# First layer's output projection with its last two column quarters computed pair by pair, the fourth quarter's weights held beside the first two slots, and a new place for the turning of each pair

## Chip, cores and metric

One core of one Trainium2 chip runs the whole program. The metric is device time in microseconds. The kernel before has a median of 3025.3 us over three runs (3021.27 to 3028.36).

## The reference, cut to what matters

The program computes two transformer layers and then a second, different block; all data are float32. The change is between the two layers of the first block. For layer l, with rows h (16 meta rows and 1024 token rows, width 1024):

```
hn   = rmsnorm(h, norm_gain[l])            # x * rsqrt(mean(x*x) + 1e-6) * gain
proj = hn @ w_in[l]                        # q, k, v, gates, forget column
...                                        # attention, gives do, fo (512 wide each)
h    = h + concatenate([do, fo]) @ w_out[l]
```

What matters here is the last line for l = 0 and the first two for l = 1: output projection, residual add, row statistics, scaling, and the first products of the next layer.

## The kernel before, in words

Five engines run five instruction streams in order. Each wait is a semaphore that a helper `Count` names by a key. **TensorE** products are done three times (high by high, high by low, low by high parts of a float32 pair), by `mm3` at L597, recorded on L595; transposes are on L604.

**Weights.** The list `PLAN` gives the order in which 512 KB slices of weights are loaded. SyncE loads slice w into one of two float32 buffers (`W32`, slot w % 2) once slice w - 2 has been split (L2702 to L2705). ScalarE writes the rounded high part (`split_to`, L1203, recorded on L1214), VectorE the low part (L1778, on L1782), each into one of two slots of `WH`, `WL`. A slot is free when the products of the slice that had it are done (`W_OVER`). Slices in `ASIDE` go elsewhere: before the change only those of a later projection, "out2", through the table `PAIRED`.

**Output projection** (`tensor_out`, L830). There are nine row tiles: eight of 128 token rows and one of 16 meta rows; two tiles make a pair p = 0 to 3, and the meta rows are pair 4. The 1024 output columns are four quarters q of 256. Each quarter has two weight slices (kk = 0, 1), each of four 128-row chunks. One tile of one slice is 12 matmuls of 128x256, so a pair of a quarter is 48, and pair 4 is 24. Quarters 0 to 2 run all nine tiles for kk = 0, then all for kk = 1. Quarter 3 runs by pairs, in `PAIR_ORDER` = 4, 0, 1, 2, 3; behind the product of place i it turns (transposes) the normalised rows of the pair of place i - 2.

**PSUM banks.** `Banks.take` (L69) gives out, of the banks allowed, the one that was taken longest ago. Who takes a bank waits for the instruction that frees it. A pair's product holds one bank, until VectorE has added it to h (`add`, L2059, recorded on L2068, for the meta rows on L2072). Turning a pair takes eight banks, one for each 128 columns (`tensor_norm_fill`, L624); bank k is freed by the k-th VectorE instruction of `norm_fill` (L1819, recorded on L1825), which runs behind ScalarE's k-th (L1254, on L1259). In quarter 3 of the kernel before, turning may not use the banks that the remaining pairs hold. In the attention, products and small steps take banks 5, 6, 7 only; 0 to 4 belong to scores.

**Normalising a pair.** When all four quarters of a pair are added: ScalarE squares and sums its two tiles and takes the root (`norm_stats`, L1247, recorded on L1226 and L1228), VectorE takes the reciprocal and scales both tiles (`norm_scale`, L1809, on L1788 and L1817), TensorE turns them, ScalarE and VectorE write the high and low parts to `AH`, `AL`. Written order: ScalarE, for each place i of `PAIR_ORDER`: statistics of place i, then the fill of place i - 1 (for i = 1 to 3). VectorE: the add of quarter 3 one place ahead, scale of place i, fill of place i - 1. The statistics are ready only one place later than the add, and the turning one more.

**Into layer 1.** `first_projections` (L376) writes the order by hand: chunk 0 of q (352 columns, needs pairs 4, 0 and 1), the fill of pair 2, chunk 0 of k, the fill of pair 3, chunks 1 and 2 of q, and so on. Position coding of a q or k chunk (`rope`) runs one matmul, one VectorE, one GpSimd and further steps beside the next products. GpSimd also stores the finished rows of h tile by tile (L2605), once quarter 3 of a pair is added.

Of the kernel before, what the change touches and what calls it, by code (L numbers as in the profile page):

```python
# [92 lines left out]
def build(nc, A, S, O):  # L93

    ctx = ExitStack()
    with ctx:
# [27 lines left out]
        with ExitStack() as first_block:  # L124
# [3 lines left out]
            QH, QL, KH, KL = (own(n, [128, 2, L], F32R) for n in ("QH", "QL", "KH", "KL"))  # L128
# [36 lines left out]
        with ExitStack() as folded_rows:  # L165
# [7 lines left out]
            EXH = spot("EXH", 22304 - 20256, [128, 2, 1024])[:, :, :]  # L173
# [73 lines left out]


        PLAN, WI = [], {}
        PAIRED = {"out2": [(EXH[:, k, :], EXL[:, k, :]) for k in range(2)], }  # L250

        def weight(key, src, split=True):
            WI[key] = len(PLAN)
# [116 lines left out]
        def chunk(g, kind, ci):  # L370
            steps = [("unit", g, kind, ci, k) for k in range(KT)]
            if kind in "qk" and g < 4:
                steps += [("late", n, (what, g, kind, ci)) for n, what in ((2, "rope"), (4, "rope_add"), (7 if g == 0 else 9, "rope_end"))]
            return steps

        def first_projections(l):  # L376

            if l == 0:
                return (chunk(0, "q", 0) + [("fill", 2), ("stats", 3)] + chunk(0, "k", 0) + chunk(0, "q", 1) + [("fill", 3)] + chunk(0, "k", 1)
                        + [("set_up",)] + chunk(0, "q", 2) + [("split", NEXT[WI[l, 0, "k"]])] + chunk(0, "k", 2) + projections(l, 0, "f") + projections(l, 0, "v"))  # L380
            return (chunk(0, "q", 0) + [("fill", 2)] + chunk(0, "k", 0) + [("fill", 3)] + chunk(0, "q", 1) + chunk(0, "q", 2)
                    + [("split", NEXT[WI[l, 0, "k"]])] + chunk(0, "k", 1) + chunk(0, "k", 2) + projections(l, 0, "f") + projections(l, 0, "v"))

        def attention_steps(l):
# [795 lines left out]
        def tensor(e):  # L1180
            banks.__init__()
            e.wait_ge(*const_in[0].at("all"))
            for p in PAIR_ORDER[:3]:
                tensor_norm_fill(e, 0, p)
            tensor_attention(e, 0)
            tensor_out(e, ("out", 0), OUT_COLS[0], lambda kt: [(o_lo, (0, kt))], lambda q, p: (out_added, (("out", 0), q, p)),
                       PAIR_ORDER, lambda i, among: tensor_norm_fill(e, 1, PAIR_ORDER[i - 2], among) if i >= 2 else None)
            tensor_attention(e, 1)
            between = {0: lambda: tensor_mod(e), 1: lambda: tensor_fill(e, "ctxrows", XC, fill_tb)}
            tensor_out(e, ("out", 1), OUT_COLS[1], lambda kt: [(o_lo, (1, kt))], lambda q, p: (out_added, (("out", 1), q, p)),  # L1190
                       after=lambda i, among: tensor_norm_fill(e, "lat", 0, among) if i == 2 else None,
                       between=lambda q: between[q]() if q in between else None)
            tensor_ctx(e)
            tensor_mixer(e)
            tensor_fourier(e)
            tensor_ffn(e)
# [3 lines left out]
        def scalar(e):  # L1200
# [46 lines left out]
            def norm_stats(l, p):  # L1247
                def ready(i):
                    t = PAIRS[p][i]
                    return [(x_in[p], PAIRS[p][-1])] if l == 0 else [(out_added, (("out", 0), 3, t // 2))]  # L1250
                t0, n = PAIRS[p][0], len(PAIRS[p])
                statistics((l, p), [N_TILES[t] for t in PAIRS[p]], ready, RSTD[:, t0:t0 + n], FIN[:, 0:1024] if (l, p) == (0, 3) else JK)
# [8 lines left out]
            def norm(l):  # L1261
                if l == 0:
                    norm_stats(0, 4)
                    norm_stats(0, 0)
                    norm_fill(0, 4)
                    norm_stats(0, 1)
                    norm_fill(0, 0)
                    split_to(WI[0, 0, "q"])
                    norm_fill(0, 1)
                    norm_stats(0, 2)  # L1270
                    split_to(WI[0, 0, "k"])
                    return
                for i, p in enumerate(PAIR_ORDER):
                    norm_stats(l, p)
                    if i == 3:
                        split_to(WI[l, 0, "k"])
                    if 1 <= i < 4:
                        norm_fill(l, PAIR_ORDER[i - 1])

            def attention(l):  # L1280
# [128 lines left out]
                        do[st[0]](*st[1:])  # L1409

            def out_splits(name):
                for q in range(4):
                    for kk in range(2):
                        split_to(WI[name, q, kk] + ((q, kk) < (3, 1)))

            def sum_h(q, p):

# [357 lines left out]
        def vector(e):  # L1775
# [52 lines left out]
            def norm(l, add=None):  # L1828

                if l == 0:  # L1830
                    norm_scale(0, 4)
                    norm_scale(0, 0)
                    norm_fill(0, 4)
                    norm_scale(0, 1)
                    norm_fill(0, 0)
                    split_to(WI[0, 0, "q"])
                    norm_fill(0, 1)
                    norm_scale(0, 2)
                    split_to(WI[0, 0, "k"])
                    return  # L1840
                add(0)
                for i, p in enumerate(PAIR_ORDER):
                    if i < 4:
                        add(i + 1)
                    norm_scale(l, p)
                    if i == 3:
                        split_to(WI[l, 0, "k"])
                    if 1 <= i < 4:
                        norm_fill(l, PAIR_ORDER[i - 1])

            def attention(l):
# [204 lines left out]
            def out(l):  # L2056
                name = ("out", l)

                def add(q, p):  # L2059
                    c = slice(256 * q, 256 * q + 256)  # L2060
                    b = banks.place.get((name, q, p), 0)
                    e.wait_ge(*out_mm.at((name, q, p)))
                    if p < 4:
                        if q == 0:
                            for t in (2 * p, 2 * p + 1):
                                e.wait_ge(*tile_in[t].at(1 + l))
                        o = HT[:, 2 * p:2 * p + 2, c]
                        e.tensor_tensor(o, o, bank(b).rearrange("p (a b) -> p a b", a=2), ALU.add).then_inc(*out_added.mark((name, q, p)))  # L2068
                    else:
                        if q == 0:  # L2070
                            e.wait_ge(*tile_in[8].at(1))
                        e.tensor_tensor(HM[0:NM, c], HM[0:NM, c], bank(b)[0:NM, 0:256], ALU.add).then_inc(*out_added.mark((name, q, p)))  # L2072

                if l == 0:
                    for q in range(4):
                        for kk in range(2):
                            split_to(WI[name, q, kk] + ((q, kk) < (3, 1)))
                        if q < 3:
                            for p in range(5):
                                add(q, p)  # L2080
                    norm(1, lambda i: add(3, PAIR_ORDER[i]))
                    return

                def gain(q, p):

                    c = slice(256 * q, 256 * q + 256)
                    o = HT[:, 2 * p:2 * p + 2, c]
                    e.wait_ge(*squared.at(("h", q, 2 * p + 1)))
                    if q == 0 and p == 0:
                        e.wait_ge(*fg_in.at(0))  # L2090
                    e.tensor_tensor(o, o, FG[:, c].unsqueeze(1).broadcast_to([128, 2, 256]), ALU.mult).then_inc(*fg_mul.mark((q, p)))

                for q in range(4):
                    if q == 1:
                        inverse("ctx", RSTD[:, 16:18])
                        e.wait_ge(*rstd.at("ctx"))
                        for t in range(2):
                            e.tensor_scalar(XC[t], XC[t], RSTD[:, 16 + t:17 + t], None, ALU.mult).then_inc(*scaled.mark(("ctxrows", t)))
                        modulation()
                    if q == 2:  # L2100
                        fill("ctxrows", [(128, 0), (128, 128)], None, TBc, CAH, CAL)
                    split_to(WI[name, q, 1])
                    if q:
                        gain(q - 1, 2)
                        gain(q - 1, 3)
                    if q < 3:
                        split_to(WI[name, q + 1, 0])
                        add(q, 0)
                        add(q, 1)
                        gain(q, 0)  # L2110
                        add(q, 2)
                        gain(q, 1)
                        add(q, 3)
                between_blocks(lambda p: add(3, p), lambda p: gain(3, p))
# [742 lines left out]
```

## Time and profile before

| what | value |
|---|---|
| median of three runs | 3025.3 us |
| the profiled execution, its own time | 3023.28 us |
| its span (first to last instruction) | 3021.5 us |
| TensorE matmul busy | 2834.5 us, 94% |
| VectorE busy | 1545.5 us, 51% |
| ScalarE busy | 1021.3 us, 34% |
| mean granted TensorE clock | 0.977 |

The time beside the span, 1.8 us, is launch and end. Times in the rows below are from the span's start. The output projection of layer 0 begins at about 807 us and layer 1's first product at 931.67 us. A timeline row gives the start, the length, engine, line and operation; in brackets stand the idle time before it and what ended that. The length of a matmul contains its pipeline, so the pace is read from start to start.

### The profile page before, as it was taken

Reading aid. Unit: us, or ns where it says so; the run is one execution under the profiler, and the core shown is the slowest. Engines: PE = TensorE matmul, PEld = TensorE weight load, DVE = VectorE, ACT = ScalarE, POOL = GpSimd, SP = SyncE. Lnnn points to the kernel's source line nnn. Section 1 sums busy time; section 2 is a strip of 40 time slices with the busy share of each in tenths; the row PEclk is TensorE's granted clock in tenths of the full one; section 3 lists DMA queues with packets and bytes.
Section 4 is the critical chain, followed back from the end, with each engine's and each line's share of the span. In section 5 each row is a group of like instructions: output and inputs, shape, how many; then the busy total and the mean of one; then the engine's idle time right before and its main releaser. Section 6 shows DMA issues by size and latency. Waiting matters only on the chain.

```text
span 3021.5 us, 43091 instructions
## 1 busy us (share of the span) xinstructions
PE 2834.5 (94%) x17460; PEld 2423.9 (80%) x17460; DVE 1545.5 (51%) x2800; ACT 1021.3 (34%) x1960; POOL 209.5 (7%) x295
## 2 busy tenths in 40 slices
PE   6899989999898889999999898999999999999999
PEld 6777777888798777877887797888898888888887
DVE  5655555545524655654455447555436444445335
ACT  5333333323214333333233355222334222223233
POOL 1000000000101100000000106000012000000000
PEclk9999999999899999999999899999999999999999
DMA  4112221120322212222221314111332111111113
GB/s 130 39 55 60 59 55 55 55 62 29 116 61 71 54 39 63 55 59 63 73 52 43 118 55 133 49 43 46 127 100 71 49 49 49 42 49 49 49 63 133
DMA packets 205397, 198.10 MB, mean 66 GB/s; under 512 B 7286, under 2 KB 181686, under 8 KB 205198
## 3 DMA queue, kind: packets, MB, share of 16 engines
q1 hardware_dynamic: 187344, 134.27, 16.8%
q0 software_dynamic: 17856, 61.07, 5.5%
q8 instruction: 141, 2.31, 0.3%
q14 instruction: 56, 0.46, 0.0%
HBM read 162.73 MB, written 32.58 MB: 65 GB/s over the span
## 4 chain that ended last, share of the span: by engine, by line
PE 79%; DVE 10%; ACT 5%; issue 4%; DMA 2%; POOL 1%; SPq 0%; ACTq 0%; DVEq 0%; POOLq 0%
PE PS L595 75%; PE PS L604 4%; DVE WL L1782 1%; DVE ST L1969 1%; DMA W<-in_w_in 1%; ACT top L1362 1%; ACT WH L1214 1%; DVE AL L1825 1%; DVE AL L2152 0%; DMA R<-in_k_fg 0%; DMA TMP<-s_os 0%; DVE V L1957 0%; DVE AL L2044 0%; DVE top L1985 0%; DVE top L1982 0%
## 5 line engine op out<-in xcount | busy, mean ns | idle before, releaser
L595 PE MATMUL PS<-AH,WH 128*128 128x512 f32 (+3 forms) x2624 | 993.7, 379 | 20.5 <-DVE AL L1825 13.8
L595 PE MATMUL PS<-AL,WH 128*128 128x512 f32 (+3 forms) x2624 | 923.6, 352 | 0.0
L595 PE MATMUL PS<-AH,WL 128*128 128x512 f32 (+3 forms) x2624 | 920.9, 351 | 0.0
L595 PEld LDWEIGHTS PS<-AH,WH 128*128 128x128 f32 x2624 | 500.5, 191 | 103.2 <-issue 21.9
L595 PEld LDWEIGHTS PS<-AL,WH 128*128 128x128 f32 x2624 | 501.4, 191 | 49.7 <-issue 1.7
L595 PEld LDWEIGHTS PS<-AH,WL 128*128 128x128 f32 x2624 | 499.9, 191 | 43.0
L1782 DVE TENSOR_TENSOR WL<-W,WH 128x1024 fp32r<-128x1024 f32 x186 | 228.5, 1230 | 325.4 <-ACT WH L1214 325.2
L595 PE MATMUL PS<-WH,AH 128*128 128x256 f32 (+1 forms) x1088 | 350.7, 322 | 11.4 <-DVE WL L1782 5.3
L595 PE MATMUL PS<-WH,AL 128*128 128x256 f32 (+1 forms) x1088 | 348.7, 320 | 0.0
L595 PE MATMUL PS<-WL,AH 128*128 128x256 f32 (+1 forms) x1088 | 348.6, 320 | 0.0
L1214 ACT ACTIVATE WH<-W 128x1024 fp32r<-128x1024 f32 x186 | 195.5, 1052 | 280.4 <-PE PS L595 256.4
L1969 DVE TENSOR_REDUCE ST<-PS 128x1 f32<-128x784 f32 (+8 forms) x272 | 187.9, 732 | 152.3 <-PE PS L595 151.8
L604 PE MATMUL PS<-ident,top 128*128 128x128 f32 (+2 forms) x1132 | 189.8, 284 | 59.1 <-issue 21.3
L595 PEld LDWEIGHTS PS<-WH,AH 128*128 128x128 f32 x1088 | 208.4, 192 | 31.2 <-DVE R L2206 5.1
L1362 ACT ACTIVATE top<-PS,ST 128x784 f32<-128x784 f32 (+8 forms) x272 | 194.2, 721 | 91.8 <-DVE ST L1969 60.2
L595 PEld LDWEIGHTS PS<-WH,AL 128*128 128x128 f32 x1088 | 208.8, 192 | 15.2
L595 PEld LDWEIGHTS PS<-WL,AH 128*128 128x128 f32 x1088 | 208.6, 192 | 15.0
L604 PEld LDWEIGHTS PS<-ident,top 128*128 128x128 f32 (+2 forms) x1132 | 133.5, 136 | 94.2 <-issue 36.9
L595 PE MATMUL PS<-top,V 128*64 128x256 f32 (+6 forms) x1176 | 187.4, 381 | 7.0 <-DVE top L2006 4.2
L595 PEld LDWEIGHTS PS<-top,V 128*64 128x64 f32 (+3 forms) x1176 | 121.3, 157 | 76.0 <-issue 44.9
L1701 ACT ACTIVATE R<-PS,R 128x512 f32<-128x512 f32 x88 | 68.5, 779 | 299.5 <-PE PS L595 299.5
L2489 DVE SCALAR_TENSOR_TENSOR R<-PS,R 128x504 f32<-128x504 f32 x88 | 65.4, 743 | 191.9 <-ACT R L1701 191.9
(326 smaller groups left out, 3243.8 us busy)
## 6 DMA issues: line engine op xcount, KB each, us to landing
W<-in_w_in SPq DMA_DIRECT2D x94, 512.0 KB, 7.7
W<-in_w_ada SPq DMA_DIRECT2D x48, 512.0 KB, 3.6
W<-in_w_up SPq DMA_DIRECT2D x44, 512.0 KB, 3.7
W<-in_w_out SPq DMA_DIRECT2D x24, 512.0 KB, 3.4
W<-in_w_down SPq DMA_DIRECT2D x22, 512.0 KB, 3.6
R<-s_xs POOLq DMA_DIRECT2D x16, 512.0 KB, 6.7
s_adap<-AST POOLq DMA_DIRECT2D x48, 128.0 KB, 7.9
top<-in_x SPq DMA_DIRECT2D x8, 512.0 KB, 9.3
```

The lines of the kernel that those rows point to most:

```text
L595: return e.matmul(out, lhsT, rhs, start=start, stop=stop, skip_group_check=True)
L604: return e.transpose(out, in_, ident[0:k, 0:k])
L1214: e.activation(high(v), W32[:, s, :], ACT.Copy).then_inc(*w_hi.mark(v))
L1362: e.activation(P[0:rows, P_SLOT[u], 0:W], PSf[0:rows, o:o + W], ACT.Exp, bias=st[:, 0:1], accum_out=st[:, 1:2]).then_inc(*exped.mark(u))
L1701: e.activation(dst[:, c:c + n], bank(b), ACT.Identity, scale=CW[:, 1, jj:jj + 1], bias=CW[:, 3, jj:jj + 1]).then_inc(*conv_a.mark((j, ab, ...
L1782: e.tensor_tensor(low(v), W32[:, slot32(v), :], f(high(v)), ALU.subtract).then_inc(*w_lo.mark(v))
L1825: e.scalar_tensor_tensor(lo, bank(b)[:, 0:n], COLS[:, 8 * l + k:8 * l + k + 1], f(hi), ALU.mult, ALU.subtract).then_inc(*fill_lo.mark((l, ...
L1969: e.tensor_reduce(ST[0:rows, ST_SLOT[u], 0:1], PSf[0:rows, o:o + W], AX.X, ALU.max, negate=True).then_inc(*row_max.mark(u))
L2489: e.scalar_tensor_tensor(d3[:, :, 1:64], o3[:, :, 0:63], CW[:, 0, jj:jj + 1], d3[:, :, 1:64], ALU.mult, ALU.add).then_inc(*conv_v.mark((j, ...
```

## The change

- `PAIRED` now also holds the projection of layer 0, with the q buffers of the attention (`QH`, `QL`, idle at that time) as the place of the two slices of quarter 3. So the order of `PLAN` for this projection becomes (0,0), (0,1), (1,0), (3,0), (1,1), (3,1), (2,0), (2,1).
- `tensor_out`, which already has the paired form, now runs quarters 2 and 3 as: pair p of quarter 2, pair p of quarter 3, then `after`. Each takes its bank just ahead of its product, out of all eight, and `after` may use all eight.
- Turning is at place i - 1 in place of i - 2, for i = 1 to 4. Pair 2 is thus turned in the projection, and its fill leaves layer 1's list.
- ScalarE and VectorE follow: VectorE adds both quarters of place i, scales it, and then fills place i - 1. The splits of layer 1's first two slices stand at place 4 between the adds of quarters 2 and 3 (ScalarE: before the statistics of place 4).

```
-        PAIRED = {"out2": [(EXH[:, k, :], EXL[:, k, :]) for k in range(2)], }
+        QHf, QLf = (x[:, :, :].rearrange("p a b -> p (a b)") for x in (QH, QL))
+        SIDES = [(QHf[:, 1024 * k:1024 * k + 1024], QLf[:, 1024 * k:1024 * k + 1024]) for k in range(2)]
+        PAIRED = {("out", 0): SIDES, "out2": [(EXH[:, k, :], EXL[:, k, :]) for k in range(2)], }
...
-            return (chunk(0, "q", 0) + [("fill", 2)] + chunk(0, "k", 0) + [("fill", 3)] + chunk(0, "q", 1) + chunk(0, "q", 2)
+            return (chunk(0, "q", 0) + chunk(0, "k", 0) + [("fill", 3)] + chunk(0, "q", 1) + chunk(0, "q", 2)
...
-                       PAIR_ORDER, lambda i, among: tensor_norm_fill(e, 1, PAIR_ORDER[i - 2], among) if i >= 2 else None)
+                       PAIR_ORDER, lambda i, among: tensor_norm_fill(e, 1, PAIR_ORDER[i - 1], among) if i else None)
...
                 for i, p in enumerate(PAIR_ORDER):
+                    if i == 4:
+                        split_to(WI[l, 0, "k"])
                     norm_stats(l, p)
-                    if i == 3:
-                        split_to(WI[l, 0, "k"])
-                    if 1 <= i < 4:
+                    if i:
                         norm_fill(l, PAIR_ORDER[i - 1])
...
             def out_splits(name):
-                for q in range(4):
-                    for kk in range(2):
-                        split_to(WI[name, q, kk] + ((q, kk) < (3, 1)))
+                split_to(WI[name, 2, 1])
...
-                add(0)
                 for i, p in enumerate(PAIR_ORDER):
-                    if i < 4:
-                        add(i + 1)
+                    add(2, p)
+                    if i == 4:
+                        split_to(WI[l, 0, "k"])
+                    add(3, p)
                     norm_scale(l, p)
-                    if i == 3:
-                        split_to(WI[l, 0, "k"])
-                    if 1 <= i < 4:
+                    if i:
                         norm_fill(l, PAIR_ORDER[i - 1])
...
                 if l == 0:
-                    for q in range(4):
-                        for kk in range(2):
-                            split_to(WI[name, q, kk] + ((q, kk) < (3, 1)))
-                        if q < 3:
-                            for p in range(5):
-                                add(q, p)
-                    norm(1, lambda i: add(3, PAIR_ORDER[i]))
+                    split_to(WI[name, 3, 0])
+                    for p in range(5):
+                        add(0, p)
+                    split_to(WI[name, 2, 0])
+                    for p in range(5):
+                        add(1, p)
+                    split_to(WI[name, 2, 1])
+                    norm(1, add)
                     return
```

## Rows read from the trace of the kernel before

**Rows 1.** The page: span, TensorE's share, the chain that ended last.

```profile
span 3021.5 us, 43091 instructions
PE 2834.5 (94%) x17460; PEld 2423.9 (80%) x17460; DVE 1545.5 (51%) x2800; ACT 1021.3 (34%) x1960; POOL 209.5 (7%) x295
...
PE 79%; DVE 10%; ACT 5%; issue 4%; DMA 2%; POOL 1%; SPq 0%; ACTq 0%; DVEq 0%; POOLq 0%
```

**Rows 2.** Stretches: busy PE, PEld, DVE, ACT, POOL, granted clock, DMA share, GB/s.

```profile
825.00:889.00 64.00, 63.69 (x538) 63.69 (x539) 15.45 (x20) 5.24 (x5) 0.00 (x0) 1.00 0.26 85
...
905.00:925.00 20.00, 16.34 (x122) 15.51 (x122) 9.57 (x27) 10.63 (x28) 2.72 (x5) 0.91 0.27 106
925.00:940.00 15.00, 10.02 (x61) 9.52 (x61) 9.92 (x20) 9.04 (x23) 1.34 (x2) 0.89 0.55 141
...
950.00:970.00 20.00, 20.00 (x122) 19.19 (x121) 9.33 (x16) 5.85 (x11) 6.38 (x5) 1.00 0.16 33
970.00:990.00 20.00, 20.00 (x131) 19.79 (x131) 9.71 (x11) 7.75 (x10) 0.00 (x0) 1.00 0.23 41
```

**Rows 3.** Timeline of TensorE around the five turnings and into layer 1.

```profile
907.35 0.37 PE L604 MATMUL PS<-ident,OTt 16*128 16x16 f32 x2 [1.38 <-DVE AL L1825]
907.65 0.51 PE L595 MATMUL PS<-WH,AH 128*128 128x256 f32 x1
...
918.02 0.36 PE L595 MATMUL PS<-WH,AH 128*128 128x256 f32 x1
...
931.67 0.66 PE L595 MATMUL PS<-AH,WH 128*128 128x352 f32 x1 [4.90 <-DVE AL L1825]
...
937.16 1.91 PE L604 MATMUL PS<-ident,V 128*128 128x128 f32 x16
939.15 0.43 PE L595 MATMUL PS<-AH,WH 128*128 128x352 f32 x1
...
940.72 0.86 PE L595 MATMUL PS<-TMP,rotm 128*128 128x352 f32 x2 [0.33 <-DVE AL L1825]
...
944.34 0.27 PE L604 MATMUL PS<-ident,GT 128*128 128x128 f32 x1
...
947.99 0.40 PE L595 MATMUL PS<-AH,WH 128*128 128x344 f32 x1 [1.74 <-DVE AL L1825]
...
1023.18 0.38 PE L604 MATMUL PS<-ident,top 128*16 128x128 f32 x2 [4.48 <-issue]
```

**Rows 4.** Timeline of VectorE: the adds of quarter 3, scalings and fills.

```profile
899.25 0.69 DVE L2068 TENSOR_TENSOR top<-top,PS 128x512 f32<-128x512 f32 x1 [5.27 <-PE PS L595]
...
904.94 0.69 DVE L2068 TENSOR_TENSOR top<-top,PS 128x512 f32<-128x512 f32 x1 [4.16 <-PE PS L595]
...
905.74 1.42 DVE L1817 TENSOR_SCALAR V<-top,SM 128x1024 f32<-128x1024 f32 x2
907.07 1.25 DVE L1825 SCALAR_TENSOR_TENSOR AL<-PS,COLS,AH 128x16 fp32r<-128x16 f32 x8
915.16 0.69 DVE L2068 TENSOR_TENSOR top<-top,PS 128x512 f32<-128x512 f32 x1 [6.84 <-PE PS L595]
...
917.30 3.22 DVE L1825 SCALAR_TENSOR_TENSOR AL<-PS,COLS,AH 128x256 fp32r<-128x256 f32 x8
924.00 0.69 DVE L2068 TENSOR_TENSOR top<-top,PS 128x512 f32<-128x512 f32 x1 [3.48 <-PE PS L595]
```

**Rows 5.** Timeline of ScalarE: statistics of pair 0 (the first and the root).

```profile
899.98 1.06 ACT L1226 ACTIVATE TMP<-top 128x1024 f32<-128x1024 f32 x1 [3.20 <-DVE top L2068]
...
902.40 0.30 ACT L1228 ACTIVATE SM<-SM 128x2 f32<-128x2 f32 x1
```

**Rows 6.** Stretches for TensorE alone: busy, granted clock, DMA share, GB/s.

```profile
907.00:908.00 1.00, 0.65 (x4) 0.88 0.85 348
...
911.00:912.00 1.00, 1.00 (x9) 0.92 0.06 20
...
1028.00:1030.00 2.00, 2.00 (x6) 0.50 0.00 0
```

## The prediction, made before the change was run

> **What bounds the kernel now.** I read the page first: TensorE is busy 94% of the span and has 79% of the chain that ended last [rows 1]. Then the stretches of this stage: inside the quarters TensorE is full (63.69 of 64 us), but around the turnings it is busy 16.34 of 20 and 10.02 of 15 us, with the granted clock at 0.91 and 0.89; from 950 us on it is full again for 40 us [rows 2]. So what this stage is worth is read from TensorE's own gaps and clock, and what TensorE loses by 948 us reaches the end, as nothing behind it has slack to take it up before 990 us. The timeline of TensorE shows the gaps, those of VectorE and ScalarE what they wait for [rows 3 to 5].
>
> **How a turning costs time before.** A turning wants eight banks and there are eight. I measure from the start of the add that follows a pair's last product to TensorE's next product. Pair 4 is turned from 904.94: the seventh turn must take again a bank that the same turning filled, and waits 1.38 us for the first fill of VectorE, which stands behind the scaling of the next pair (905.74, 1.42 us); next product 907.65, so 2.71 us [rows 3, 4]. Pair 0: 915.16 to 918.02, 2.86 us. Pair 1: 924.00 to 931.67, 7.67 us; layer 1's first chunk needs all eight fills, and two splits stand ahead of them. Pair 2, in layer 1: 937.16 to 939.15 and then 0.33 of wait, 2.3 us. Pair 3: 944.34 to 947.99, 3.65 us, 1.74 of it a wait for the fill that frees a bank. Sum **19.2 us**. The clock fell to half (1.2 of 2.4 GHz) after the turning of pair 4 and came back in 911 to 912; the 48 matmuls there took 7.51 us (907.65 to 915.16) where a pair takes 5.69 (899.25 to 904.94): about 1.65 us lost [rows 3, 4, 6]. After the gap of 4.90 us the same: the mean clock of 0.89 over 15 us is 1.65 us of work lost [rows 2]. In both together **3.3 us**.
>
> **Part 1: the order of products and weights.** The number of products is the same: two quarters, 4.5 pairs each at 5.69 us, 51.2 us. The extra waits for weights on each tile are on semaphores long passed; I take 0.2 us in all. The two slices of quarter 3 are split during quarter 1 and the loads shift by one place. VectorE's adds of quarter 0 wait behind the split of (3,0), some microseconds; TensorE asks for a bank of quarter 0 only at the fourth pair of quarter 1, three pairs of 12 matmuls a tile after its start (8.5 us), so I cost that at nothing; a load later than that would be waited for (rival d). The short wait for the second slice ahead of the first by-pairs quarter (pair 4 gives only 12 matmuls of cover for one split of ScalarE and one of VectorE) moves from quarter 3 to quarter 2 and keeps its price. The slices of layer 1 come earlier. GpSimd's stores of h keep their place behind each pair. Nothing gained, nothing lost: **+0.2 us**.
>
> **Part 2: turning one place sooner.** This is where the change decides. Behind the products of place i TensorE turns place i - 1 into all eight banks, and the next product takes the bank taken longest ago: the first of that turning. It is freed by VectorE's first fill. That fill stands on VectorE behind the adds and the scaling of place i, and this scaling needs ScalarE's statistics of place i, which can begin only when TensorE has just ended place i. Before, the statistics of a place ran beside the next place's products; now they are in front of it. The chain from the add's start a, from rows of pair 0: ScalarE starts at a + 0.73 (899.98 - 899.25), root at a + 3.15 (902.40) [rows 4, 5]; the reciprocal 0.3 later and the scaling 0.2 behind that, as between 904.94 + 0.69 and 905.74 nothing else is slow; scaling to the first fill takes 1.33 (905.74 to 907.07) [rows 4]. So the first fill starts at a + 5.0. A small fill is 0.16, a large one 0.40 (3.22 / 8), and TensorE follows 0.04 later. Products resume at **a + 5.25** behind the turning of pair 4, and at **a + 5.46** behind those of pairs 0 and 1. Sixteen turns are 1.9 us [rows 3], so the idle time is 3.6 us, and 4.4 behind pair 4.
>
> **Part 3: into layer 1.** Pair 2 is turned at place 4, again into eight banks. Chunk 0 of q may use 5, 6, 7 only. I followed the order in which banks are taken from the end of the attention (2, 1, 4, 0, 3, then the three others): the turning of pair 2 begins with bank 3, and its second bank is the first of the three. So chunk 0 waits for the second fill: a + 5.0 + 0.81 + 0.04 = **a + 5.87**, in place of 7.67 before. Its weights are split beside pair 3 of quarter 3 and are early. Then chunk 0 of k follows at once, and pair 3 is turned: 3.65 us as before, plus up to 0.6, since ScalarE's end of the position coding of q now falls on the end of chunk k, without the turning of pair 2 between them: 4.25.
>
> **The sum.** After: 5.25 + 5.46 + 5.46 + 5.87 + 4.25 = 26.3 us; before 19.2; **+7.1 us**. The clock: four gaps of 3.6 to 4.4 us with TensorE idle where before it fell twice. The gap of 4.90 was followed by half clock, that of 1.74 was not (the stretch at 950 us is at 1.00) [rows 2, 3]; mine are nearer the first. Two more falls at 1.65: **+3.3 us**. With part 1, +10.6; I take **+10**, as the 0.6 at pair 3 may not come. The profiled execution took 3023.3 us, so 3033; it stood 2 us under the median of 3025.3, and the median should go to about **3035**.
>
> The Trainium skill, "TensorE: Matmul & The Clock Gate", section "HAM oscillation — how this bites in real kernels", says that a gap repeated in every step is paid again in every step, since the array restarts at half clock each time. By it all four gaps would bring a fall, the 3.3 us above; the two gaps at 907 and 931 us agree, that each of the new ones does so no row can show yet.
>
> **Rivals.** (a) *Turning is hidden, faster.* Banks rotate, and the fills of a turning run beside the next products. Then only the turns themselves stay: 0.9 + 1.9 + 1.9 + 1.9 + 4.25 = 10.9 us in place of 19.2, and no clock falls: -8.3 - 3.3 = -11.6, so 3013.7. (0.9 for the small turning: its last bank waits for the add, 0.69 us [rows 4].) It decides if the first fill can start within the 1.9 us of the turns, or break-even if it starts about 2.5 us sooner than a + 5.0. Against it: ScalarE's two squares alone last from a + 0.73 to a + 3.15, and the wait of 1.38 us at 907.35 shows that a bank not yet filled from does stop TensorE. Chance 0.06. The Trainium skill's "Perfetto Trace Analysis", section "Optimizing Tensor Performance", says that product groups should rotate through different banks so that emptying one overlaps the next; by it the change would go this way. The same page, "Identifying Performance Opportunities", reads the same gap repeating on the bounding engine as too little PSUM for the next tile; that speaks against the change, and the wait at 907.35 agrees.
>
> (b) *The clock falls no more often than before, or layer 1 takes some up.* +3 to +6.6: 3028 to 3032. For it: a fall needs not follow each gap. The chunks to 990 us leave no slack [rows 2], later stalls might. Chance 0.17.
>
> (c) *Half clock lasts twice as long.* After the 4.48 us gap at 1023.18 the clock was still 0.50 in 1028 to 1030 [rows 3, 6]. If that happens in each of four gaps, +6.6 more: about 3042. Chance 0.12.
>
> (d) *The new order of weights starves quarter 1.* A late (3,0) delays VectorE's adds; it must be over 8 us late. +2 us or more; chance 0.03.
>
> (My forecast: the remaining 0.62.) What a measurement of this kernel can tell from no change is 0.2%, 6 us. Slower than that: the forecast, (c), (d), and a small part of (b): 0.77. Within it: most of (b): 0.15. Faster: (a) and a little for what I don't see: 0.08. Range: the low end takes in (b) nearly whole, 3027; the high end (c), 3043. Left out are (a) and the ends.
>
> **What would show it.** Right: TensorE idle 3.5 to 4.5 us three times between its pairs, each ended by VectorE's L1825, with half clock after each; ScalarE's squares of a pair at the same time as TensorE's turns of the pair before; layer 1's chunk 0 of q starting 5.9 us behind the last add; the stretch from the end of quarter 1 to chunk 1 of q about 10 us longer than before. Wrong: gaps under 2 us there (then rival a), or the stage longer by 10 us and the whole not (then something later had slack).

## The result, and the profile after

The changed kernel is **slower by 0.39%**: the ratio to the kernel before is 1.0039, 95% interval 1.0028 to 1.0049; medians of seven runs each are 3034.9 and 3023.1 us. The profiled execution took 3035.3 us against 3023.3, 12.0 us more. The page of the kernel after shows the same work in a longer span, with TensorE's busy time almost as before (2835.9 against 2834.5 us); helpers moved by two lines (products are now recorded on L597, turning on L606).

```profile
span 3033.5 us, 43095 instructions
PE 2835.9 (93%) x17460; PEld 2428.1 (80%) x17460; DVE 1545.2 (51%) x2800; ACT 1021.3 (34%) x1960; POOL 209.0 (7%) x295
```

The page can't say where 12 us went. The stretches can. These are the kernel after, cut at the ends of its pairs (busy time of PE, PEld, DVE, ACT, POOL, then granted clock, DMA share, GB/s):

```profile
882.00:902.00 20.00, 15.44 (x113) 15.16 (x112) 4.64 (x14) 3.91 (x13) 1.09 (x2) 0.83 0.13 53
902.00:922.00 20.00, 16.17 (x115) 15.94 (x114) 6.13 (x14) 5.50 (x13) 1.05 (x2) 0.83 0.13 53
922.00:941.00 19.00, 15.17 (x118) 14.93 (x117) 8.56 (x16) 7.71 (x16) 1.05 (x2) 0.91 0.22 68
941.00:960.00 19.00, 13.22 (x74) 12.54 (x72) 8.66 (x21) 9.49 (x24) 1.99 (x3) 0.82 0.33 98
960.00:990.00 30.00, 29.77 (x180) 28.79 (x181) 10.91 (x20) 7.32 (x15) 6.53 (x5) 1.00 0.15 36
```

Four stretches of 19 to 20 us in a row, each with 3.8 to 5.8 us in which TensorE does nothing, and each with a mean clock of 0.82 to 0.91. Before, two stretches looked so [rows 2]. TensorE's timeline names what ended each gap:

```profile
887.48 0.58 PE L597 MATMUL PS<-WH,AH 128*128 128x256 f32 x1 [4.31 <-DVE AL L1825]
901.26 1.91 PE L606 MATMUL PS<-ident,V 128*128 128x128 f32 x16
906.99 0.58 PE L597 MATMUL PS<-WH,AH 128*128 128x256 f32 x1 [3.83 <-DVE AL L1825]
...
926.96 0.58 PE L597 MATMUL PS<-WH,AH 128*128 128x256 f32 x1 [3.83 <-DVE AL L1825]
...
946.06 0.63 PE L597 MATMUL PS<-AH,WH 128*128 128x352 f32 x1 [4.26 <-DVE AL L1825]
...
953.07 0.75 PE L597 MATMUL PS<-TMP,rotm 128*128 128x352 f32 x2
...
956.58 0.27 PE L606 MATMUL PS<-ident,GT 128*128 128x128 f32 x1
...
960.23 0.40 PE L597 MATMUL PS<-AH,WH 128*128 128x344 f32 x1 [1.74 <-DVE AL L1825]
```

Each gap is ended by L1825, VectorE's fill, the instruction that gives a bank of the turning back. VectorE's own timeline shows why it comes so late, and ScalarE's shows what it waits for in turn:

```profile
863.90 0.41 DVE L2071 TENSOR_TENSOR OTt<-OTt,PS 16x256 f32<-16x256 f32 x1 [0.73 <-PE PS L597]
...
882.19 0.69 DVE L2067 TENSOR_TENSOR top<-top,PS 128x512 f32<-128x512 f32 x1 [4.98 <-PE PS L597]
885.66 0.17 DVE L1788 RECIPROCAL SM<-SM 128x2 f32<-128x2 f32 x1 [2.78 <-ACT SM L1230]
885.86 1.42 DVE L1817 TENSOR_SCALAR V<-top,SM 128x1024 f32<-128x1024 f32 x2
887.20 1.22 DVE L1825 SCALAR_TENSOR_TENSOR AL<-PS,COLS,AH 128x16 fp32r<-128x16 f32 x8
...
901.46 0.69 DVE L2067 TENSOR_TENSOR top<-top,PS 128x512 f32<-128x512 f32 x1 [4.98 <-PE PS L597]
...
906.46 3.22 DVE L1825 SCALAR_TENSOR_TENSOR AL<-PS,COLS,AH 128x256 fp32r<-128x256 f32 x8
...
921.42 0.69 DVE L2067 TENSOR_TENSOR top<-top,PS 128x512 f32<-128x512 f32 x1 [4.98 <-PE PS L597]
...
940.08 0.69 DVE L2067 TENSOR_TENSOR top<-top,PS 128x512 f32<-128x512 f32 x1 [2.21 <-PE PS L597]
```

```profile
882.91 1.06 ACT L1228 ACTIVATE TMP<-top 128x1024 f32<-128x1024 f32 x1 [8.88 <-DVE top L2067]
...
885.34 0.29 ACT L1230 ACTIVATE SM<-SM 128x2 f32<-128x2 f32 x1
885.54 1.41 ACT L1261 ACTIVATE AH<-PS,COLS 128x16 fp32r<-128x16 f32 x8
```

Read them together. Pair 0's last product ends at 882.19, the add starts; ScalarE had been idle for 8.88 us and begins the squares only at 882.91; VectorE waits 2.78 us for the root, scales for 1.4 us, and only then (887.20) fills the pair turned before. TensorE resumes at 887.48. From each add to the next product: 5.29, 5.53 (901.46 to 906.99), 5.54 and 5.98 us (940.08 to 946.06). Behind the turning of pair 3 it is 3.65 us, as before.

I call **stage** the stretch from the last add of quarter 1 to the first product of chunk 1 of q. After, it is 960.23 - 863.90 = 96.33 us. Before, that add starts at 863.94 and the chunk at 947.99 [rows 3], 84.05 us. The stage is longer by 12.3 us, the execution by 12.0: within that difference of 0.3 us, the loss is all here.

### The profile page after: what moved, and what is told of

It reads as the page before. It is cut to its first block, busy times and chain, and to the rows that moved or that the text cites. A ratio compares the mean times of both kernels' runs of the same rounds, so it can differ in the third digit from the quotient of the medians.

```text
span 3033.5 us, 43095 instructions
## 1 busy us (share of the span) xinstructions
PE 2835.9 (93%) x17460; PEld 2428.1 (80%) x17460; DVE 1545.2 (51%) x2800; ACT 1021.3 (34%) x1960; POOL 209.0 (7%) x295
## 4 chain that ended last, share of the span: by engine, by line
PE 79%; DVE 9%; ACT 5%; issue 4%; DMA 2%; POOL 1%; SPq 0%; ACTq 0%; DVEq 0%; POOLq 0%
PE PS L597 75%; PE PS L606 4%; DMA W<-in_w_in 2%; DVE ST L1968 1%; DVE WL L1782 1%; ACT top L1364 1%; ACT WH L1216 1%; DVE AL L2152 0%; ACT TMP L1228 0%; DVE AL L1825 0%; DMA R<-in_k_fg 0%; DMA TMP<-s_os 0%; DVE V L1956 0%; DVE top L1984 0%; DVE AL L2043 0%
## 5 line engine op out<-in xcount | busy, mean ns | idle before, releaser
L597 PE MATMUL PS<-AH,WH 128*128 128x512 f32 (+3 forms) x2624 | 992.9, 378 | 19.8 <-DVE AL L1825 13.1
L597 PE MATMUL PS<-AL,WH 128*128 128x512 f32 (+3 forms) x2624 | 923.6, 352 | 0.0
L597 PE MATMUL PS<-AH,WL 128*128 128x512 f32 (+3 forms) x2624 | 921.8, 351 | 0.0
L597 PEld LDWEIGHTS PS<-AH,WH 128*128 128x128 f32 x2624 | 500.6, 191 | 101.4 <-issue 21.0
L597 PEld LDWEIGHTS PS<-AL,WH 128*128 128x128 f32 x2624 | 501.5, 191 | 49.5 <-issue 1.2
L597 PEld LDWEIGHTS PS<-AH,WL 128*128 128x128 f32 x2624 | 499.9, 191 | 43.0
L597 PE MATMUL PS<-WH,AH 128*128 128x256 f32 (+1 forms) x1016 | 333.0, 328 | 24.0 <-DVE AL L1825 12.0
L597 PE MATMUL PS<-WH,AL 128*128 128x256 f32 (+1 forms) x1016 | 330.5, 325 | 0.0
L597 PE MATMUL PS<-WL,AH 128*128 128x256 f32 (+1 forms) x1016 | 330.5, 325 | 0.0
L606 PE MATMUL PS<-ident,top 128*128 128x128 f32 (+2 forms) x1132 | 190.0, 284 | 61.0 <-issue 23.6
L597 PEld LDWEIGHTS PS<-WH,AH 128*128 128x128 f32 x1016 | 197.4, 194 | 44.3 <-DVE AL L1825 12.5
L606 PEld LDWEIGHTS PS<-ident,top 128*128 128x128 f32 (+2 forms) x1132 | 134.4, 137 | 95.2 <-issue 39.0
L597 PEld LDWEIGHTS PS<-WH,AL 128*128 128x128 f32 x1016 | 197.4, 194 | 15.2
L597 PEld LDWEIGHTS PS<-WL,AH 128*128 128x128 f32 x1016 | 197.4, 194 | 15.0
L597 PE MATMUL PS<-top,V 128*64 128x256 f32 (+6 forms) x1176 | 187.5, 381 | 7.0 <-DVE top L2005 4.2
L597 PEld LDWEIGHTS PS<-top,V 128*64 128x64 f32 (+3 forms) x1176 | 121.4, 158 | 76.1 <-issue 45.1
```

Source lines behind the costliest of these rows:

```text
L597: return e.matmul(out, lhsT, rhs, start=start, stop=stop, skip_group_check=True)
L606: return e.transpose(out, in_, ident[0:k, 0:k])
```

## The experiments

All are compared with the kernel before by the ratio of their times, and by their stage, read as above from one profiled execution each. The edits are shown against the changed kernel, cut ("...") and with some lines told in a comment.

| kernel | ratio, 95% interval | stage, us |
|---|---|---|
| before | 1 | 84.05 |
| changed | 1.0039 (1.0028 to 1.0049) | 96.33 |
| e1, by pairs, turned two places behind | 1.0003 (0.9995 to 1.0012) | 84.13 |
| e2, fill first | 0.9961 (0.9950 to 0.9973) | 70.74 |
| e3, two blocks to a bank | 0.9956 (0.9944 to 0.9968) | 68.69 |
| e4, turned again | 1.0024 (1.0015 to 1.0033) | 91.04 |
| e5, fill first on VectorE only | 1.0020 (1.0010 to 1.0031) | 90.05 |
| e6, banks reserved | 1.0040 (1.0026 to 1.0053) | 97.05 |
| e7, turned between | 0.9955 (0.9942 to 0.9967) | 70.62 |
| e8, between, two to a bank | 0.9952 (0.9940 to 0.9965) | 68.23 |

The stage's difference and the whole's agree within about 2 us in each: what is lost or won here reaches the end.

**e1: is it the order of products and weights, or the turning?** TensorE turns place i - 2 again, and the order on ScalarE and VectorE and the place of layer 1's splits follow the kernel before:

```
-  ... chunk(0, "q", 0) + chunk(0, "k", 0) + [("fill", 3)] ...
+  ... chunk(0, "q", 0) + [("fill", 2)] + chunk(0, "k", 0) + [("fill", 3)] ...
-  tensor_norm_fill(e, 1, PAIR_ORDER[i - 1], among) if i else None
+  tensor_norm_fill(e, 1, PAIR_ORDER[i - 2], among) if i >= 2 else None
   # VectorE: adds of both quarters one place ahead; splits at place 3 behind scale and statistics
```

> Part 1 of the change alone: quarters 2 and 3 by pairs and the weights in q's place, but turning stays two places behind, the fill of pair 2 stays in layer 1 and VectorE adds one place ahead, as before the change. If the loss is all in turning one place sooner, this takes as long as the kernel before, within 2 us (resumes at about 2.4 and 2.7 us behind the add, 7.7 into layer 1). If the new order of products and weights costs something itself, it is slower than before by more than 3 us.

Ratio 1.0003. TensorE's waits in e1 (engine and line, who was waited for: us in total, times, longest):

```profile
PE PS L597 <- DVE AL L1825: 10.1, 4, 6.0
PE PS L597 <- DVE WL L1782: 1.0, 1, 1.0
```

In the changed kernel the first of these rows has 18.0 us in five waits:

```profile
PE PS L597 <- DVE AL L1825: 18.0, 5, 4.3
```

So q's place for the weights, the new order of loads and the pairs of two quarters together cost nothing that can be measured. All the loss is in turning one place sooner, with the order on ScalarE and VectorE that goes with it. The equality is one of sums. In e1 products resume 2.41 and 2.66 us behind the turnings of pairs 4 and 0, a little sooner than before (2.71 and 2.86), 7.67 into layer 1 as before, and the half clock behind that last gap lasts longer (mean clock 0.85 in 922 to 932 and 0.80 in 932 to 942, against 0.98 and 0.85). So e1 bounds the cost of the new order of products and weights to about 1 us, an estimate from these differences, and not to 0.1.

**e2: the order on ScalarE and VectorE.**

```
   # in both engines, at each place i
-  norm_stats(l, p)            # VectorE: norm_scale(l, p)
   if i:
       norm_fill(l, PAIR_ORDER[i - 1])
+  norm_stats(l, p)            # VectorE: norm_scale(l, p)
```

> The changed kernel with one edit: at each place ScalarE and VectorE do the fill of the pair before ahead of the statistics and the scaling of the new pair. Theory (the gap is statistics and scaling standing in front of the fill that frees a bank): products resume 2.0 us behind the add in place of 5.3 to 5.5, layer 1's chunk 0 at 2.0 in place of 6.0, no half clock in the stage; 15 us less idle and some 9 us less at half clock, so about 24 us under the changed kernel and 12 under the one before, 3011. Rival (the fills themselves, 3.0 us on ScalarE and 3.2 on VectorE, are too slow for eight banks): products resume at 4 us or later, and at most 6 us are won.

The stage is 25.6 us shorter than the changed kernel's, ratio 0.9961 to the kernel before. TensorE, ScalarE and VectorE at the second turning:

```profile
892.89 1.91 PE L606 MATMUL PS<-ident,V 128*128 128x128 f32 x16
894.55 0.37 PE L597 MATMUL PS<-WH,AH 128*128 128x256 f32 x1
```

```profile
893.30 3.03 ACT L1261 ACTIVATE AH<-PS,COLS 128x256 fp32r<-128x256 f32 x8 [8.56 <-PE PS L606]
896.18 1.11 ACT L1228 ACTIVATE TMP<-top 128x1024 f32<-128x1024 f32 x1
```

```profile
893.09 0.69 DVE L2067 TENSOR_TENSOR top<-top,PS 128x512 f32<-128x512 f32 x1 [4.98 <-PE PS L597]
893.81 3.23 DVE L1825 SCALAR_TENSOR_TENSOR AL<-PS,COLS,AH 128x256 fp32r<-128x256 f32 x8
```

The fill starts 0.7 us behind the add in place of 5.0, and products resume at 1.46 us in place of 5.53, without a wait. That is even less than the 2.0 expected: the turning itself begins before the add. Into layer 1 it is 1.71 us (919.27 to 920.98). The granted clock is 1.00 in every stretch from 864 to 972, so the half clock is gone with the gaps. ScalarE's squares now follow the fill, beside the next products, where they hold up nobody. The rival (fills too slow for eight banks) falls: they take 3.0 and 3.2 us but the first of them frees its bank before TensorE asks for it.

**e3: are all eight banks part of it?** A turning puts blocks k and k + 1 into one bank, ScalarE and VectorE read them there; statistics and scaling still come first.

```
-  each = 1 if l in (0, 1) else 2
+  each = 1 if l == 0 else 2
   # the fills: bank of the even block, columns from 256 * (k % 2),
   # VectorE waits for ScalarE's part of both blocks
```

> The changed kernel with its order of work, but a turning puts two blocks of 128 columns into one bank, so it takes four banks in place of eight; ScalarE and VectorE still do statistics and scaling first. Theory (TensorE stops only because all eight banks are taken): products resume 2 us behind the add though the fills still start at 5 us, and some 20 to 24 us are won against the changed kernel. Rival (the order on ScalarE and VectorE alone sets the gap, whatever the banks): products still resume at about 5.5 us and nothing is won.

```profile
892.91 1.91 PE L606 MATMUL PS<-ident,V 128*128 128x128 f32 x16
894.57 0.37 PE L597 MATMUL PS<-WH,AH 128*128 128x256 f32 x1
```

```profile
893.11 0.69 DVE L2069 TENSOR_TENSOR top<-top,PS 128x512 f32<-128x512 f32 x1 [4.98 <-PE PS L597]
...
898.11 2.05 DVE L1827 SCALAR_TENSOR_TENSOR AL<-PS,COLS,AH 128x256 fp32r<-128x256 f32 x5
```

VectorE's fill still starts 5.0 us behind the add (898.11), yet TensorE goes on at 1.46 us, sooner than the 2 expected. Ratio 0.9956; the stage is 27.6 us shorter than the changed kernel's, more than the 20 to 24 expected, and 1.7 us of that is the wait behind the turning of pair 3 in layer 1, which is gone too. So the gap needs both: a late fill, and a turning that holds every bank. Taking away either one takes away the gap.

**e4: the clock.** Work is added to fill the gap: the transposes of pairs 0, 1, 2 are done twice, those of pair 4 six times, into the same place.

```
+  for again in range(1 if l != 1 or p == 3 else 6 if p == 4 else 2):
       for i, x in enumerate(tiles):
```

> The changed kernel with work added in the gap: in the projection each transpose of pairs 0, 1 and 2 is done twice, those of pair 4 six times, into the same place. The products still resume at 5.3 to 5.5 us behind the add, but TensorE idles 1.9 us in place of 3.8. If the idle time brings the half clock, the pairs behind the gaps run at their 11.4 us again in place of 13.1 to 14.4, and the whole is 7 to 9 us faster than the changed kernel, though it does more. If the half clock has another cause, or costs nothing in the end, the time is that of the changed kernel or up to 6 us more.

```profile
881.89 3.32 PE L606 MATMUL PS<-ident,OTt 16*128 16x16 f32 x48
...
906.36 0.38 PE L597 MATMUL PS<-WH,AH 128*128 128x256 f32 x1 [2.08 <-DVE AL L1826]
...
923.55 0.38 PE L597 MATMUL PS<-WH,AH 128*128 128x256 f32 x1 [2.08 <-DVE AL L1826]
...
941.19 0.40 PE L597 MATMUL PS<-AH,WH 128*128 128x352 f32 x1 [2.52 <-DVE AL L1826]
```

```profile
884.00:886.00 2.00, 1.20 (x17) 0.67 0.91 367
886.00:888.00 2.00, 0.72 (x3) 0.50 0.39 158
...
906.00:908.00 2.00, 1.64 (x13) 1.00 0.03 8
...
944.00:946.00 2.00, 2.00 (x9) 0.50 0.04 16
```

The columns of the second fence are TensorE's busy time, granted clock, DMA share and GB/s. With 2.08 us of gap in place of 3.83, the clock stayed at 1.00 (2.4 GHz) behind the turnings of pairs 0 and 1, and the 96 products there took 11.65 and 11.66 us (906.36 to the add at 918.01, 923.55 to 935.21) in place of 14.43 and 13.12. It still fell to 0.50 (1.2 GHz) around the turning of pair 4 and within layer 1's first chunk, behind a gap of 2.52 us. The fall at pair 4 does not follow the gap there (885.2 to 887.28, 2.08 us): the mean of 0.67 over 884 to 886 puts it at about 884.7, while the 48 small transposes (881.89 to 885.21) still ran. The kernel does more and is faster than the changed one: 5.3 us in the stage, 4.5 us by the ratios, whose intervals touch, so the stage is the firmer number. That is under the 7 to 9 us expected, because two of the four falls stayed: 13.54 us for the place behind pair 4 (887.28 to the add at 900.82) is still 1.9 over 11.65.

**e5: how the 5 us are made up.** Only VectorE's order is that of e2; ScalarE keeps statistics first.

> The changed kernel with half of e2: only VectorE does its fill ahead of the scaling; ScalarE keeps its statistics in front of its own fill. By the chain (statistics end at 3.4 us behind the add, then ScalarE's first fill, then VectorE's) products resume at 3.9 us behind large turnings and 3.7 behind the small one, in place of 5.5 and 5.3: 6.5 us less idle over four gaps, and one or two half clocks fewer, so 7 to 11 us under the changed kernel, near the one before. If ScalarE's part alone set the gap (the scaling was hidden), nothing is won; if VectorE's alone, as much as in e2.

```profile
885.40 0.39 PE L597 MATMUL PS<-WH,AH 128*128 128x256 f32 x1 [2.95 <-DVE AL L1825]
...
902.97 0.38 PE L597 MATMUL PS<-WH,AH 128*128 128x256 f32 x1 [2.67 <-DVE AL L1825]
```

The adds start at 881.48 and 898.59, so products resume at 3.92 and 4.38 us; I had said 3.7 and 3.9. The chain that I wrote down had ScalarE's first fill and then VectorE's behind statistics that end at 3.4 us, but 3.9 has room for only one of the two. Of the 5.53 us behind a large turning, VectorE's scaling in front was 1.15, ScalarE's statistics in front 2.9 (4.38 to e2's 1.46), and 1.46 is the turning and its start. The ratio, 1.0020, is 5.7 us under the changed kernel, less than the 7 to 11 expected. Products resumed 4.9 us sooner in sum, not 6.5, and the two gaps of 2.67 us, like those of 2.95 and 3.11, were still followed by half clock.

**e6: is it the choice of banks?** The banks of the next pair's two products are taken ahead of the turning, which then has six.

```
+  if name == ("out", 0) and i < 4:
+      hold(2, order[i + 1])
+      hold(3, order[i + 1])
-  after(i, ALL)
+  after(i, [b for b in ALL if b not in the two just held])
```

> The changed kernel with the banks of the next pair's two products taken ahead of the turning, which then has six, as the kernel before had in its last quarter. If stopping TensorE is a matter of which instruction takes the last bank, this helps: products resume at 2 us. If it is that the first fill starts only at 5.0 us, whoever needs a bank waits for it: now the seventh turn, and products resume at 5.8 us or so, 0 to 2 us slower than the changed kernel.

```profile
885.40 0.42 PE L606 MATMUL PS<-ident,OTt 16*128 16x16 f32 x2 [4.32 <-DVE AL L1830]
904.24 1.11 PE L606 MATMUL PS<-ident,V 128*128 128x128 f32 x4 [4.27 <-DVE AL L1830]
```

Now the transposes wait (L606), for the same instruction and no shorter than the products did (4.32 and 4.27 us against 4.31 and 3.83). Products resume 5.64 and 6.31 us behind the add, where 5.8 was expected; the ratio is 1.0040 and the stage 0.7 us longer than the changed kernel's. It is the late fill that counts, not who takes the last bank. This is the wait of 1.38 us at 907.35 in the kernel before [rows 3], grown by the statistics.

**e7 and e8: a version that beats both.** Fill first, and a pair is turned between the next pair's two quarters (`middle`), where its scaling is just done; e8 adds two blocks to a bank.

```
-  PAIR_ORDER, lambda i, among: tensor_norm_fill(...) if i else None)
+  PAIR_ORDER, middle=lambda i: tensor_norm_fill(e, 1, PAIR_ORDER[i - 1]) if i else None)
   # VectorE: add(2, p), fill of place i - 1, [splits], add(3, p), norm_scale(l, p)
```

> A version meant to be faster: fill first as in e2, and each pair is turned between the next pair's quarter 2 and quarter 3, 5.7 us behind its own last product, when its scaling (5.0 us) is just done. No turning is left behind the last product, so layer 1's chunk 0 starts at once. Four turnings still cost TensorE 0.5 to 1.9 us each. Expected: e2's time or 0 to 3 us less, 3007 to 3010; if the scaling comes too late, a wait of under 1 us at each turning.

> e7 with e3's two blocks to a bank. Banks are then short nowhere: the wait of 1.7 us for a bank behind the turning of pair 3 in layer 1 goes too. Expected 1 to 2 us under e7, about 14 us under the kernel before. If banks were not what was waited for there, the time of e7.

```profile
888.65 1.91 PE L606 MATMUL PS<-ident,V 128*128 128x128 f32 x16
...
934.27 0.40 PE L597 MATMUL PS<-AH,WH 128*128 128x344 f32 x1 [1.74 <-DVE AL L1825]
```

The place is right by a hair: in e7 the scaling of pair 0 starts at 886.84 and lasts 1.42 us, and its turning starts at 888.65 without a wait. Ratios 0.9955 and 0.9952. The stage is 0.12 us shorter than that of e2 (70.62), so the place wins nothing over e2; e8's two blocks to a bank win 2.4 us in the stage, among them the 1.74 us wait that the row above still shows. e2, e3, e7 and e8 can't be told apart by their ratios, whose intervals overlap; all four beat both kernels. e2 and e3 are the smallest steps from the changed kernel: e2 moves one line on each of two engines, e3 keeps the order and packs the banks.

## Why the prediction was right, point by point

- **Part 1 at +0.2 us.** e1 shows it: 84.13 us of stage against 84.05. The late split of (3,0) that rival (d) feared held up nothing; TensorE's one wait for weights in the stage is 0.99 us, as before, one quarter sooner.
- **Part 2, the chain behind the add.** Said: fill from a + 5.0, products at a + 5.25 and 5.46. Measured: the fill at 5.01 and 5.00, products at 5.29, 5.53, 5.54. e2 and e5 show the two parts of the chain, e3 the banks' part. The rows of the kernel before held all of it, because the same instructions ran there in another order.
- **Part 3, layer 1.** Said a + 5.87, measured 5.98, so the bank found by following the order of taking was right. Behind pair 3 I had 4.25, "up to 0.6" more than before; it was 3.65. The end of q's position coding did not get in the way.
- **The turnings together.** Said 26.3 against 19.2, +7.1. Measured 5.29 + 5.53 + 5.54 + 5.98 + 3.65 = 26.0, +6.8.
- **The clock, mis-sized.** This is the term of the sum that was off by most. Said two more falls at 1.65 us, +3.3. There were two more, but they cost more each. A full-clock place takes 11.66 us (e4); the three places behind gaps took 13.98, 14.43 and 13.12, so 2.3, 2.8 and 1.5 us lost. Chunk 0 of q (24 products, 0.161 us each at full clock, 4.0 with the start) took 6.0 (946.06 to the rope matmul at 953.07, less six products of k in front of it), 2.0 lost. Sum 8.6 us. Before, on the same measure, 1.5 at 907.65 to 915.16 and 1.5 in chunk 0: 3.0. The term is +5.6 and not +3.3. With 6.8 it makes 12.4, where the stage measured 12.3.
- **Why it was mis-sized.** I had priced a fall by its shortest examples. Reckoned from the means of stretches of 1 and 2 us, the half clock lasted about 3.4 us in both falls before (some 907.8 to 911.1 and 931.6 to 935.0), and in the changed kernel about 6.8 us in three and 3.4 in one. So what rival (c) assumed, twice as long, came true in three of four, but its +6.6 us did not: up to 2 us of each half-clock stretch lay over idle time, where it costs nothing, and a product at half clock starts every 0.213 us in place of 0.119 and not at twice the time. Of its 6.6 us, 2.0 came (8.6 against the forecast's 6.6). The second 1.65 us was read from a mean clock over a stretch with idle time in it; it fitted because that fall began only with the products.
- **The total.** Said +10, from a sum of +10.6; measured +12.0. The turnings were 0.3 us too high and the clock 2.3 too low, and part 1 cost nothing that can be measured. The larger term was right, and that kept the total near.
- **Rival (a)** needed the first fill within the 1.9 us of the turns. It starts at 5.0. But its price was nearly right for a kernel in which the turning is hidden: e2 is 0.39% under the kernel before, 11.8 us, and e3 0.44%, 13.3 us, where the rival said 11.6. The closeness is in part luck, as it priced the turning of pair 3 at 4.25 us, and e2 has 3.65 there.
- **Rival (b)** falls: all four gaps had a fall in them or right behind them, and nothing later took the loss up. The changed kernel's 12.3 us in the stage is 12.0 at the end.

The Trainium skill's "TensorE: Matmul & The Clock Gate", section "HAM oscillation — how this bites in real kernels", says that a repeated gap pays for a slow restart each time. The changed kernel's trace agrees with that for its gaps of 3.8 to 4.3 us, four of four; e4's two of 2.08 us kept the clock. By the Trainium skill's "Perfetto Trace Analysis", section "Optimizing Tensor Performance", groups rotating through banks are to hide the emptying. Here that holds in e2 and e3 and not in the changed kernel, so the measurement adds a condition: where one turning takes every bank, the emptying must not stand behind work that waits for the group just finished.

## What to carry to other kernels

When TensorE's output takes all the banks, the next product waits for the first emptying instruction, so look at what stands ahead of that on its in-order engine: anything there that depends on TensorE's latest product puts its whole latency into the path. Either empty first and do the new work after, or leave banks free. Price a gap of TensorE not only by its length but by the half clock behind it: here 8.6 us beside 16.2 us of idle time in the four gaps.

## What the hardware did that I had not expected

The half clock began inside the long gaps or at their end and outlasted them by different times. In the 4.31 us gap it was there from 886 on, with TensorE still idle, and in 892 to 894 the mean was 0.82; the loss per gap was 1.5 to 2.8 us for gaps of nearly one length. The difference is how long the half clock lay over products. The two gaps of 3.83 us show it: behind the first the clock was back only within 912 to 914, behind the second within 930 to 932, that is about 6.2 and 3.3 us after the products resumed, and they lost 2.8 and 1.5 us. Why one lasted twice as long as the other, no run shows. Columns: TensorE's busy time, granted clock, DMA share, GB/s.

```profile
884.00:886.00 2.00, 0.00 (x0) 0.97 0.81 324
886.00:888.00 2.00, 0.52 (x2) 0.50 0.49 201
...
892.00:894.00 2.00, 2.00 (x16) 0.82 0.00 0
...
912.00:914.00 2.00, 2.00 (x14) 0.70 0.00 0
...
930.00:932.00 2.00, 2.00 (x18) 0.93 0.00 0
```

And the length of the gap alone does not tell whether the clock falls. In e4, 2.08 us behind 32 transposes of 128x128 kept the full clock, twice; in e5, 2.67 us behind 16 of them did not. Gaps of 0.95 us (e1) and 1.74 us (layer 1, in the kernels before and after and in e2) kept it, but around the small transposes of pair 4 it fell with less: with gaps of 0.43 and 1.38 us in the kernel before, with 1.44 us in e1, and in e4 while they were still running. What makes the difference was not tried.
